# Reordered first loads and copies, later memory turns, two modulation units in the cross attention, and a low part between two norm tiles

## The chip, the cores and the metric

One core of a Trainium2 chip runs the whole program. The time is the device time of one execution in microseconds; the median of several executions is compared. Engines are TensorE (PE, with its weight loads PEld), VectorE (DVE), ScalarE (ACT), GpSimd (POOL) and SyncE (SP), which here only issues transfers.

## The reference

The program computes three transformer blocks on 256 tokens of width 1024, all in float32. Two layers of the first kind come first, then one of the second kind:

```python
for l in range(2):
    h = rms_norm(x, pre_mix_g[l])
    x = x + rms_norm(parallel_mixer(h, ...), post_mix_g[l])      # LRU, 8 forgetting heads, 4 retention heads
    h = rms_norm(x, pre_cross_g[l])
    x = x + rms_norm(memory_cross_attention(h, mem_n, ...), post_cross_g[l])   # mem_n = rms_norm(mem, mem_norm_g)
    h = rms_norm(x, pre_ffn_g[l])
    x = x + rms_norm(swiglu(h, w_gate[l], w_up[l], w_down[l]), post_ffn_g[l])
mod = silu(c) @ w_ada + b_ada        # six vectors of 1024 that shift, scale and gate the last block
...                                  # windowed attention and spatial gating, then 16 experts, 32 tokens each
```

The vector `mod` needs nothing of x. Its matrix of 1024 x 6144 is read during the first two layers.

## The kernel before, in words

**Units.** In the first half the weights come in units of 128 x 2048 floats (1 MiB). A unit goes through four hands. SP loads it into one of four slots W (L2335, `load_unit`). ScalarE copies it to the format of the fast product, the high part WH (L974). VectorE subtracts that from W, which gives the low part WL (L1493). TensorE multiplies: activations too are kept as a high and a low part, and each product is three (high by high, high by low, low by high), 48 of 256 columns or 24 of 512 to a unit. WH and WL have two buffers each, so the high part of unit m waits until TensorE is done with unit m - 2. A slot is free again once the low part is made.

**Order.** No scheduler runs: each engine has its own program, and the order is what the Python code of that engine calls. `unit()` on ScalarE and VectorE makes the parts of the present and the next unit, if they aren't made (`ahead`), and then advances the side jobs by two steps (`beside.step(2)`); TensorE advances them by one step after each half of a unit. A side job is a generator; each `yield` ends its step. Two lanes run side by side: one has the forget gates and then the recurrence, the other the parameters (8 steps) and then the norm and turning of the memory (`norming`, L402, L1022, L1538). A step of one engine can wait for the same job's step on another, and everything that follows on that engine waits too.

**Norms.** A norm of X is: squares with row sums (ScalarE), mean square (VectorE), its power -1/2 (GpSimd), scaling of each of two 128-row tiles, half by VectorE and half by ScalarE, then 16 transposes on TensorE (L398 in steps, L422 at once), whose results ScalarE and VectorE store as high and low parts (L1019, L1488), eight chunks each. `post_norm` (L1547) does the other side for each tile: y times gain, times the root, plus X (L1557, L1488). It is followed by one to four units of keys or values of the memory (`FILL`, `norm_after`), beside which the next norm runs.

**Start.** SP issues X, the identity, the parameters, units 0, 1 and 2, three small tables (positions, forget bias, sink), the other constants, the memory, and then unit 3 and on. ScalarE does squares, scaling, the high parts of units 0 and 1 (`high(0)`, `early()`), and then the stores of the turned norm, for which it needs the parameters. VectorE waits for the identity and makes the one-hot column (two casts), then does its part of the norm, the low part of unit 0, and the low parts of the norm.

**Cross attention** (L644, L1241, L1885). Four query units, then four output units `w_co`. Around them go the scores of heads 0 to 3 (i = 0 to 3), their turning one step later, and the product with the values two steps later. VectorE does the maxima and probabilities of head i, then, for i of 4 and 5, two steps of `modulation` each, then the low parts of the units, then the low half of the values' result.

**Modulation** (L1564). Twelve of the 24 units of `w_ada_2` per layer are handled on VectorE: one multiplication and seven multiply-adds of 128 x 256 elements, in four steps of two. Loads go to two buffers AW and wait until the unit two before is done (L2346). They stand in SP's queue between the weight units: units 0 and 1 of a layer in the cross attention, unit n + 2 after the n-th feed-forward step. Unit 0 of a layer is computed in the cross attention, unit n + 1 in feed-forward step n: two of the eight operations after each of two weight units, two between the halves of the hidden product and two before its second half (L1923; from step 2 on another weight unit comes in between).

**Second half.** The experts' weights come in 192 loads of 2816 KB into six buffers. They are not split in parts. The first six wait for places in memory that the first half frees, the others for the buffer's last product.

Of the kernel before, what the change touches and what calls it, by code (L numbers as in the profile page):

```python
# [62 lines left out]
NW = 4  # L63
# [241 lines left out]
def tensor_program(e, C):  # L305
# [93 lines left out]
            ins.then_inc(*up("full", "turn", name, k0))  # L399
            yield  # L400

    def norming(name, rows=M.XN1):  # L402
        yield
        e.wait_ge(*at("scaled_first", name, 1))
        e.wait_ge(*at("scaled_second", name, 1))
        yield from turning(name, [rows[:, 0, :], rows[:, 1, :]], 8)
# [58 lines left out]
    def mixer(l):  # L465
# [31 lines left out]
        proj_t("w_in", l, 1, HT, ("ly", l))  # L497
        fg, rec = forget(), recurrence()
        beside.add(fg, rec)
        memory = norming(("mem",), M.XN)  # L500
        if l == 0:
            beside.add(parameters(), memory, lane=1)
        proj_t("w_in", l, 2, HT, ("q", l, 0))
# [199 lines left out]
    def ffn(l):  # L703
# [17 lines left out]
        ada_sum(12 * l + 11)  # L721
        down(10)

    pre_norm(("mix", 0))
    for l in range(2):
        mixer(l)
# [230 lines left out]
def scalar_program(e, C):  # L957
# [8 lines left out]
    def par(name, i=0, n=1):  # L966
        a = PC[name][0] + i
        return M.PT[:, a:a + n]
# [13 lines left out]
    def early():  # L982
        m = here + 1
        if m < len(units) and m not in done:
            high(m)
# [33 lines left out]
                e.activation(dst[0][:, first + k, :], ps[:, k - k0, :], ACT.Identity, scale=g).then_inc(*up("hi", name, k))  # L1019
            yield  # L1020

    def norming(name, gain, ready, src=X, dst=HT, rows=M.XN1):  # L1022
        squares(name, src, ready)
        yield
        scaled(name, src, rows)
        yield from turning(name, dst, 0, 8, gain)

    def run_all(job):
# [61 lines left out]
    def mixer(l):  # L1090
# [63 lines left out]
        fg, rec = forget(), recurrence()  # L1154
        beside.add(fg, rec)
        if l == 0:
            memory = norming(("mem",), par("mem", 0, 8), ("mem",), M.XN, MEM, M.XN)
            beside.add(parameters(), memory, lane=1)
        unit()
        q_out(0)  # L1160
# [147 lines left out]
    scaled(("mix", 0))  # L1308
    high(0)
    here = 0  # L1310
    early()
    e.wait_ge(*at("par"))
    run_all(turning(("mix", 0), HT, 0, 8, par("pre_mix0", 0, 8)))
    for l in range(2):
        mixer(l)
        post_squares(("mix", l))
        norm_after(("post_mix", l), norming(("cross", l), par(f"pre_cross{l}", 0, 8), ("x", "mix", l)), l)
        cross(l)
        post_squares(("cross", l))
        norm_after(("post_cross", l), norming(("ffn", l), par(f"pre_ffn{l}", 0, 8), ("x", "cross", l)), 1)  # L1320
        ffn(l)
        post_squares(("ffn", l))
        if l == 0:
            norm_after(("post_ffn", 0), norming(("mix", 1), par("pre_mix1", 0, 8), ("x", "ffn", 0)), 1)
# [140 lines left out]
def vector_program(e, C):  # L1465
# [69 lines left out]
            ins.then_inc(*freed("turn", name, k0))  # L1535
            yield

    def norming(name, gain, dst=HT, *rows):  # L1538
        norm_head(name, *rows)
        yield  # L1540
        yield from turning(name, dst, 0, 8, gain)

    def run_all(job):
        for _ in job:
            pass

    def post_norm(y, gain, src=None, tmp=M.TMP):  # L1547
        for t in range(2):
            for h in range(2):
                if h:  # L1550
                    mean_square(y, at("ysq", *y, t, 1), t, "pms")
                else:
                    e.wait_ge(*at("ysq", *y, t, 0))
                c = slice(512 * h, 512 * h + 512)
                i = PS[:, 2 * t + h, :] if src is None else src[:, t, c]
                g = gain[:, c]
                e.tensor_tensor(tmp[:, t, c], i, g, ALU.mult).then_inc(*up("yfree", *y, t, h))  # L1557
            e.wait_ge(*at("prs", *y, t))
            for h in range(2):
                c = slice(512 * h, 512 * h + 512)  # L1560
                e.wait_ge(*at("yfree", *y, t, h))
                stt(X[:, t, c], tmp[:, t, c], K["rs2"][:, t:t + 1], X[:, t, c], ALU.mult, ALU.add).then_inc(*up("x", *y, t, h))
# [116 lines left out]
    def mixer(l):  # L1679
# [86 lines left out]
        fg, rec = forget(), recurrence()  # L1766
        beside.add(fg, rec)
        if l == 0:
            memory = norming(("mem",), par("mem", 0, 8), MEM, M.XN, M.XN)
            beside.add(parameters(), memory, lane=1)  # L1770
        for _ in range(3):
            unit()
# [112 lines left out]
    def cross(l):  # L1885
        def scores(h):
            P, col = M.PP[h % 3], 2 * h
            ps = two(full("cs", l, h))
            e.tensor_reduce(K["mxx"][:, col:col + 2], ps, AX.X, ALU.max).then_inc(*step())
            own()  # L1890
            ts(K["nmx"][:, col:col + 2], K["mxx"][:, col:col + 2], -1.0, None, ALU.mult).then_inc(*up("cnmx", l, h))
            e.wait_ge(*free("cs", l, h))
            e.reciprocal(K["rcp"][:, col:col + 2], K["sms"][:, col:col + 2]).then_inc(*step())
            own()
            for t in range(2):
                o = P[:, 256 * t:256 * t + 256]
                ins = ts(o, o, K["rcp"][:, col + t:col + t + 1], None, ALU.mult)
            ins.then_inc(*up("cprobs", l, h))

        def values(h):  # L1900
            ps = two(full("co", l, h))
            e.wait_ge(*at("co_high", l, h))
            e.tensor_tensor(MX[1][:, 2 * h:2 * h + 2, :], ps, MX[0][:, 2 * h:2 * h + 2, :].bitcast(F32), ALU.subtract).then_inc(
                *freed("co", l, h))

        unit()
        job = modulation(12 * l)
        for i in range(6):
            if i < 4:
                scores(i)  # L1910
            else:
                next(job)
                next(job)
            if i + 1 < 4:
                unit()
            if i >= 4:
                unit()
            if i >= 2:
                values(i - 2)
        unit()  # L1920
        unit()

    def ffn(l):  # L1923
        for n in range(11):
            A, i = M.A[n % 2], n % 4
            job = modulation(12 * l + n + 1)
            unit()
            next(job)
            ada_sum(12 * l + n)
# [15 lines left out]
        ada_sum(12 * l + 11)  # L1945
        unit()

    e.wait_ge(*at("id"))
    for i in range(2):
        ins = e.tensor_copy(M.ONE[64 * i:64 * i + 64, :], M.ID[0:64, 0:8])  # L1950
    ins.then_inc(*up("one_hot"))
    nrm = norming(("mix", 0), par("pre_mix0", 0, 8))
    next(nrm)
    low(0)
    e.wait_ge(*at("par"))
    run_all(nrm)
    for l in range(2):
        mixer(l)
        e.wait_ge(*at("gb", "mix", l))
        post_norm(("mix", l), M.GB)  # L1960
        norm_after(("post_mix", l), norming(("cross", l), par(f"pre_cross{l}", 0, 8)))
        cross(l)
        e.wait_ge(*at("gb", "cross", l))
        post_norm(("cross", l), M.GB)
        norm_after(("post_cross", l), norming(("ffn", l), par(f"pre_ffn{l}", 0, 8)))
        ffn(l)
        e.wait_ge(*at("gb", "ffn", l))
        post_norm(("ffn", l), M.GB)
        if l == 0:
            norm_after(("post_ffn", 0), norming(("mix", 1), par("pre_mix1", 0, 8)))  # L1970
# [360 lines left out]
def sync_program(e, C, out):  # L2331
# [20 lines left out]
    for t in range(2):  # L2352
        e.dma_start(M.X[:, t, :], D["x"][0, 128 * t:128 * t + 128, :]).then_inc(*up(f"x{t}", by=16))
        for h in range(2):
            same(("x", t, h), (f"x{t}",))
    e.dma_start(M.CST[:, 0:128], D["consts"][:, 0:128]).then_inc(*up("id", by=16))
    e.dma_start(M.PT[:, :], D["params"]).then_inc(*up("par", by=16))
    for m in range(NW - 1):
        load_unit(m)
    e.dma_start(K["posf"].bitcast(I32), D["positions_t"]).then_inc(*up("sm", 0, by=16))  # L2360
    e.dma_start(K["bf"][0:8, :], D["fox_b_t"]).then_inc(*up("sm", 1, by=16))
    e.dma_start(K["snk"], D["sink_2"].broadcast_to([128, 8])).then_inc(*up("sm", by=16))
    e.dma_start(M.CST[:, 128:NCONST], D["consts"][:, 128:NCONST]).then_inc(*up("cst", by=16))
    for t in range(2):
        e.dma_start(M.XN[:, t, :], D["mem"][0, 128 * t:128 * t + 128, :]).then_inc(*up(f"mem{t}", by=16))
# [141 lines left out]
```

## Time and profile before

| | us |
|---|---|
| median of three runs | 2382.78 (2379.72 to 2384.42) |
| the profiled execution, its own time | 2379.06 |
| its span, first to last instruction | 2377.3 |
| TensorE busy | 1824.5 (77%) |
| VectorE busy | 808.5 (34%) |
| ScalarE busy | 531.3 (22%) |
| chain that ended last | DMA 49%, TensorE 41%, VectorE 5% |

A line of the profile says: busy time of a group, its mean in ns, then the idle time of the engine just before it and what ended that idle time. In the timeline, "[3.65 <-issue]" means that the engine did nothing for 3.65 us and then began with no releaser that the profile shows. "WL<-W,WH" is output and inputs.

### The profile page before, as it was taken

The numbers are of one execution on the slowest core, as the hardware profiler recorded it, in microseconds if no ns is written. First come the engines' busy times: TensorE is split into PE (matmuls) and PEld (weight loads), VectorE is DVE, ScalarE is ACT, GpSimd is POOL, SyncE is SP. The second block draws the span as 40 slices with busy tenths as digits, with TensorE's granted clock in tenths as the row PEclk, the third lists the DMA queues.
The fourth block names the chain that finished last, engine by engine and source line by source line (L and its number), as shares of the span: only waits on it lengthen the run. The fifth ranks groups of instructions, "written<-read, shape, count | busy, mean of one in ns | idle before, by whom it ended". The sixth has DMA issues, their size and how long they took to land.

```text
span 2377.3 us, 28602 instructions
## 1 busy us (share of the span) xinstructions
PE 1824.5 (77%) x12548; PEld 1178.4 (50%) x12548; DVE 808.5 (34%) x1229; ACT 531.3 (22%) x800; POOL 90.8 (4%) x140
## 2 busy tenths in 40 slices
PE   7998999999988998977666566666656665566665
PEld 6888889988888997864121111122111121111121
DVE  4655667656556777653010101001100110010002
ACT  5634533355454434441000000000000000000000
POOL 1200000012000000010000000000000000000000
PEclk9999999999999999977877788788877877877777
DMA  7345467754454776347999999999999999999996
GB/s 241 107 135 194 142 213 238 240 163 134 142 165 154 249 246 204 125 188 323 429 429 430 429 429 429 429 429 430 429 429 429 430 430 428 428 430 429 428 429 265
DMA packets 171067, 739.78 MB, mean 311 GB/s; under 512 B 6672, under 2 KB 133136, under 8 KB 146240
## 3 DMA queue, kind: packets, MB, share of 16 engines
q1 hardware_dynamic: 168592, 731.27, 77.3%
q0 software_dynamic: 2352, 6.69, 0.8%
q8 instruction: 99, 1.62, 0.3%
q14 instruction: 24, 0.20, 0.0%
HBM read 736.88 MB, written 1.05 MB: 310 GB/s over the span
## 4 chain that ended last, share of the span: by engine, by line
DMA 49%; PE 41%; DVE 5%; ACT 2%; issue 2%; POOL 1%; SPq 0%; POOLq 0%; DVEq 0%; ACTq 0%
PE PS L325 39%; DMA WB<-in_w_down 24%; DMA WB<-in_w_up 23%; DVE WL L1493 1%; ACT WH L974 1%; DVE X L1488 1%; DMA W<-in_w_gate 1%; POOL T L2234 1%; DVE C L1488 1%; DMA S<-in_post_mix_g 1%; PE PS L398 0%; DMA W<-in_w_in 0%; PE PS L422 0%; DVE S L1557 0%; DVE S L1488 0%
## 5 line engine op out<-in xcount | busy, mean ns | idle before, releaser
L325 PE MATMUL PS<-WB,XS 128*32 128x352 f32 x3072 | 363.5, 635 | 211.3 <-DMA WB<-in_w_up 124.2
L325 PE MATMUL PS<-WB,S 128*32 128x512 f32 x1408 | 268.8, 759 | 156.5 <-DMA WB<-in_w_down 78.8
L1493 DVE TENSOR_TENSOR WL<-W,WH 128x2048 fp32r<-128x2048 f32 x141 | 322.9, 2290 | 146.1 <-ACT WH L974 146.0
L325 PEld LDWEIGHTS PS<-WB,XS 128*32 128x32 f32 x3072 | 115.6, 141 | 456.6 <-issue 177.9
L1488 DVE SCALAR_TENSOR_TENSOR S<-S,PS 128x352 f32<-128x352 f32 (+1 forms) x110 | 63.3, 587 | 784.8 <-ACT S L1458 751.2
L325 PE MATMUL PS<-HTh,WH 128*128 128x256 f32 x1064 | 310.5, 292 | 18.8 <-DVE HTl L1488 8.4
L974 ACT ACTIVATE WH<-W 128x2048 fp32r<-128x2048 f32 x141 | 268.8, 1908 | 199.7 <-PE PS L325 186.7
L325 PE MATMUL PS<-HTl,WH 128*128 128x256 f32 x1064 | 305.0, 287 | 0.0
L325 PE MATMUL PS<-HTh,WL 128*128 128x256 f32 x1064 | 304.9, 287 | 0.0
L325 PEld LDWEIGHTS PS<-WB,S 128*32 128x32 f32 x1408 | 72.1, 127 | 342.2 <-issue 222.2
L325 PEld LDWEIGHTS PS<-HTh,WH 128*128 128x128 f32 x1064 | 208.3, 196 | 21.8 <-DVE WL L1493 10.4
L325 PEld LDWEIGHTS PS<-HTl,WH 128*128 128x128 f32 x1064 | 208.3, 196 | 1.0
L325 PEld LDWEIGHTS PS<-HTh,WL 128*128 128x128 f32 x1064 | 208.1, 196 | 0.0
L1453 ACT ACTIVATE S<-PS 128x256 f32<-128x256 f32 x16 | 6.1, 384 | 850.0 <-PE PS L887 850.0
L2223 DVE TENSOR_TENSOR N<-N,PS 128x512 f32<-128x512 f32 x60 | 41.2, 687 | 368.4 <-PE PS L325 368.4
L325 PE MATMUL PS<-C,XS 128*32 128x352 f32 x1024 | 111.5, 590 | 65.9 <-DMA C<-in_w_up 37.9
L325 PE MATMUL PS<-WH,MXh 128*128 128x512 f32 x336 | 134.5, 400 | 2.0 <-DVE MXl L1488 2.0
L325 PE MATMUL PS<-WL,MXh 128*128 128x512 f32 x336 | 132.0, 393 | 0.0
L325 PE MATMUL PS<-WH,MXl 128*128 128x512 f32 x336 | 132.0, 393 | 0.0
L325 PE MATMUL PS<-S 128*128 128x512 f32 (+3 forms) x288 | 102.8, 490 | 30.3 <-DVE S L2210 22.1
L325 PEld LDWEIGHTS PS<-C,XS 128*32 128x32 f32 x1024 | 36.5, 132 | 139.2 <-DMA C<-in_w_up 52.5
L1461 ACT ACTIVATE S<-PS 128x512 f32<-128x512 f32 x16 | 9.6, 597 | 378.1 <-PE PS L325 378.1
(269 smaller groups left out, 2105.3 us busy)
## 6 DMA issues: line engine op xcount, KB each, us to landing
WB<-in_w_down SPq DMA_DIRECT2D x64, 2816.0 KB, 36.0
WB<-in_w_gate SPq DMA_DIRECT2D x48, 2816.0 KB, 35.9
WB<-in_w_up SPq DMA_DIRECT2D x48, 2816.0 KB, 35.9
C<-in_w_gate SPq DMA_DIRECT2D x16, 2816.0 KB, 36.2
C<-in_w_up SPq DMA_DIRECT2D x16, 2816.0 KB, 37.2
W<-in_w_in SPq DMA_DIRECT2D x31, 1024.0 KB, 5.4
S<-in_w_ada SPq DMA_DIRECT2D x24, 1024.0 KB, 5.4
W<-in_w_gate SPq DMA_DIRECT2D x22, 1024.0 KB, 7.8
```

The costliest lines, as they stand in the source:

```text
L325: return e.matmul(o, l, r, start=start, stop=stop, skip_group_check=True)
L974: e.activation(M.WH[m % 2][:, :], M.W[:, 2048 * (m % NW):2048 * (m % NW) + 2048], ACT.Copy).then_inc(*up("high", m))
L1453: e.activation(M.SG[ex % 2], ps[:, 0:256], ACT.Copy).then_inc(*freed("sg", ex))
L1461: e.activation(M.DN[ex % 2][:, 0, :], PS[:, 4, :], ACT.Copy).then_inc(*up("dn0", ex))
L1488: return e.scalar_tensor_tensor(out=o, in0=a, scalar=s, in1=b, op0=o1, op1=o2)
L1493: e.tensor_tensor(M.WL[i][:, :], M.W[:, 2048 * (m % NW):2048 * (m % NW) + 2048], M.WH[i][:, :].bitcast(F32), ALU.subtract).then_inc(*up("l ...
L2223: e.tensor_tensor(o, o, ps, ALU.add).then_inc(*done_)
L2234: return e.tensor_tensor(o, i, K["mhalf"] if n == 1 else K["mhalf"].broadcast_to([128, n]), ALU.pow)
```

## The change

Five edits. (1) Start: SP issues unit 0 ahead of the parameters, the three small tables next, then waits for unit 0's landing before it issues units 1 and 2. ScalarE's `early()` (unit 1's high part) comes after the stores of the turned norm. VectorE's one-hot casts come after the norm's head and unit 0's low part. TensorE waits for the identity itself. (2) The memory's norm has two more empty steps between scaling and the first turning, on all three engines. (3) In layer 0, VectorE's `post_norm` after the mixer makes the low parts of the present and the next unit between its two tiles. (4) In the cross attention two modulation units are computed, two steps at each of i = 2, 3 (first unit) and 4, 5 (second). (5) In return feed-forward step 0 has none; steps 1 to 10 keep theirs. The order of the modulation loads in SP's queue is the same.

```diff
 # TensorE
-    def norming(name, rows=M.XN1):
-        yield
+    def norming(name, rows=M.XN1, pad=0):
+        for _ in range(1 + pad):
+            yield
-        memory = norming(("mem",), M.XN)
+        memory = norming(("mem",), M.XN, 2)
+    e.wait_ge(*at("id"))
     pre_norm(("mix", 0))
 # ScalarE
         squares(name, src, ready)
         yield
         scaled(name, src, rows)
+        for _ in range(pad):
+            yield
         yield from turning(name, dst, 0, 8, gain)
-            memory = norming(("mem",), par("mem", 0, 8), ("mem",), M.XN, MEM, M.XN)
+            memory = norming(("mem",), par("mem", 0, 8), ("mem",), M.XN, MEM, M.XN, 2)
     high(0)
-    early()
     e.wait_ge(*at("par"))
     run_all(turning(("mix", 0), HT, 0, 8, par("pre_mix0", 0, 8)))
+    early()
 # VectorE
-    def post_norm(y, gain, src=None, tmp=M.TMP):
+    def post_norm(y, gain, src=None, tmp=M.TMP, between=None):
         for t in range(2):
+            if t and between:
+                between()
-            memory = norming(("mem",), par("mem", 0, 8), MEM, M.XN, M.XN)
+            memory = norming(("mem",), par("mem", 0, 8), MEM, M.XN, M.XN, pad=2)
-        job = modulation(12 * l)
+        jobs = [modulation(12 * l + i) for i in range(2)]
         for i in range(6):
             if i < 4:
                 scores(i)
-            else:
-                next(job)
-                next(job)
+            if i >= 2:
+                for _ in range(2):
+                    next(jobs[i // 2 - 1])
-            job = modulation(12 * l + n + 1)
+            job = modulation(12 * l + n + 1) if n else iter(range(4))
+    nrm = norming(("mix", 0), par("pre_mix0", 0, 8))
+    next(nrm)
+    low(0)
     e.wait_ge(*at("id"))
     for i in range(2):
         ins = e.tensor_copy(M.ONE[64 * i:64 * i + 64, :], M.ID[0:64, 0:8])
     ins.then_inc(*up("one_hot"))
-    nrm = norming(("mix", 0), par("pre_mix0", 0, 8))
-    next(nrm)
-    low(0)
-        post_norm(("mix", l), M.GB)
+        post_norm(("mix", l), M.GB, between=None if l else ahead)
 # SP
     e.dma_start(M.CST[:, 0:128], D["consts"][:, 0:128]).then_inc(*up("id", by=16))
+    load_unit(0)
     e.dma_start(M.PT[:, :], D["params"]).then_inc(*up("par", by=16))
-    for m in range(NW - 1):
-        load_unit(m)
     (the three small tables)
+    e.wait_ge(*at("w0", 0))
+    for m in range(1, NW - 1):
+        load_unit(m)
```

## Rows read from the trace of the kernel before

**Rows 1.** Page, the span in 40 slices: busy tenths of TensorE and DMA.

```profile
PE   7998999999988998977666566666656665566665
DMA  7345467754454776347999999999999999999996
```

**Rows 2.** Chain of waits, 0 to 1100 us: start us, us, what.

```profile
190.14 14.66 PE PS L325 x120
306.52 8.02 DMA W<-in_w_gate
```

**Rows 3.** Timeline of ScalarE at the start: start us, us, instruction, count, idle before.

```profile
10.25 1.91 ACT L974 ACTIVATE WH<-W 128x2048 fp32r<-128x2048 f32 x1 [1.05 <-DMA W<-in_w_in]
13.26 1.91 ACT L974 ACTIVATE WH<-W 128x2048 fp32r<-128x2048 f32 x1 [1.10 <-DMA W<-in_w_in]
15.08 3.01 ACT L1019 ACTIVATE HTh<-PS,PT 128x256 fp32r<-128x256 f32 x8
```

**Rows 4.** Timeline of VectorE at the start.

```profile
5.98 0.34 DVE L1950 CAST ONE<-C 64x8 fp32r<-64x8 f32 x2 [5.98 <-DMA C<-in_consts]
...
12.19 2.29 DVE L1493 TENSOR_TENSOR WL<-W,WH 128x2048 fp32r<-128x2048 f32 x1 [3.23 <-ACT WH L974]
16.06 3.23 DVE L1488 SCALAR_TENSOR_TENSOR HTl<-PS,PT,HTh 128x256 fp32r<-128x256 f32 x8 [1.58 <-ACT HTh L1019]
```

**Rows 5.** Page, DMA issues: count, KB each, median us from issue to landing.

```profile
W<-in_w_in SPq DMA_DIRECT2D x31, 1024.0 KB, 5.4
```

**Rows 6.** Timeline of TensorE: its first product and five gaps in mid-stream.

```profile
17.08 0.55 PE L325 MATMUL PS<-HTh,WH 128*128 128x256 f32 x1 [5.61 <-DVE HTl L1488]
...
83.76 1.09 PE L398 MATMUL PS<-C,N 128*128 128x128 f32 x4 [3.65 <-issue]
...
190.14 0.39 PE L325 MATMUL PS<-WH,MEMh 128*128 128x256 f32 x1 [2.65 <-DVE WL L1493]
...
311.52 0.39 PE L325 MATMUL PS<-HTh,WH 128*128 128x256 f32 x1 [2.10 <-DVE WL L1493]
327.72 0.39 PE L325 MATMUL PS<-HTh,WH 128*128 128x256 f32 x1 [2.51 <-DVE WL L1493]
...
761.16 0.39 PE L325 MATMUL PS<-HTh,WH 128*128 128x256 f32 x1 [1.36 <-DVE WL L1493]
```

**Rows 7.** Stretches, TensorE alone: us, busy (x), granted clock, DMA share, GB/s.

```profile
83.40:86.80 3.40, 3.04 (x15) 0.50 0.86 283
312.10:315.50 3.40, 3.40 (x18) 0.50 1.09 350
```

**Rows 8.** Timelines of ScalarE and VectorE around the norm after mixer 0.

```profile
182.37 1.91 ACT L974 ACTIVATE WH<-W 128x2048 fp32r<-128x2048 f32 x1
...
189.03 1.90 ACT L974 ACTIVATE WH<-W 128x2048 fp32r<-128x2048 f32 x1
...
187.80 2.28 DVE L1493 TENSOR_TENSOR WL<-W,WH 128x2048 fp32r<-128x2048 f32 x1
...
192.43 2.28 DVE L1493 TENSOR_TENSOR WL<-W,WH 128x2048 fp32r<-128x2048 f32 x1
```

**Rows 9.** Timelines of VectorE and ScalarE in the cross attention of layer 0.

```profile
252.85 2.29 DVE L1493 TENSOR_TENSOR WL<-W,WH 128x2048 fp32r<-128x2048 f32 x1 [0.51 <-ACT WH L974]
...
257.64 0.60 ACT L1268 ACTIVATE MXh<-PS 128x512 fp32r<-128x512 f32 x1 [4.82 <-PE PS L325]
```

**Rows 10.** Timelines of VectorE and ScalarE in feed-forward step 0, layer 0.

```profile
304.04 2.04 DVE L1488 SCALAR_TENSOR_TENSOR C<-S,T,C 128x256 f32<-128x256 f32 x4
...
306.71 0.63 ACT L1301 ACTIVATE MXh<-S 128x512 fp32r<-128x512 f32 x1 [7.08 <-DVE S L1488]
...
314.56 1.91 ACT L974 ACTIVATE WH<-W 128x2048 fp32r<-128x2048 f32 x1 [5.42 <-DMA W<-in_w_gate]
```

**Rows 11.** Timeline of VectorE beside GpSimd work in the mixer of layer 0.

```profile
105.74 1.33 DVE L1485 TENSOR_SCALAR C<-C,T 128x128 f32<-128x128 f32 x2
...
109.83 0.29 DVE L1782 CUSTOM_DVE_ANT_0 C<-PS,C 128x128 f32<-128x128 f32 x1 [0.77 <-PE PS L325]
```

More of the change, by code:

```diff
@@ L1020, in turning, with norming @@
             yield
-    def norming(name, gain, ready, src=X, dst=HT, rows=M.XN1):
+    def norming(name, gain, ready, src=X, dst=HT, rows=M.XN1, pad=0):
         squares(name, src, ready)
@@ L1536, in turning, with norming @@
             yield
-    def norming(name, gain, dst=HT, *rows):
+    def norming(name, gain, dst=HT, *rows, pad=0):
         norm_head(name, *rows)
-        yield
+        for _ in range(1 + pad):
+            yield
         yield from turning(name, dst, 0, 8, gain)
```

## The prediction

> **What bounds the kernel now.** I read the page's slices first. From the 20th of 40 slices (1130 us) DMA is 9 tenths busy or more and TensorE 5 to 7; before, TensorE is mostly at 8 or 9 tenths and DMA at 3 to 7 [rows 1]. So the second half streams expert weights, and its start is set by TensorE's progress in the first half; a microsecond won before 1089 us should arrive whole at the end, because every expert load waits for a buffer that earlier work frees. Then I read the chain of waits for the first 1100 us. It is TensorE work (a long piece is shown), broken by short stretches that are not: two are the landing of a gate load, 8.0 us each, one per layer, of which the first is shown [rows 2]. Last, TensorE's own timeline: the idle ahead of its first product and of five later ones [rows 6]. The sum is over these gaps.
>
> **1. First unit.** ScalarE makes the high part of unit 0 when the load lands (10.25 to 12.16), then waits 1.10 us for unit 1, makes its high part, and only at 15.08 begins the turned norm [rows 3]. VectorE finishes the low part of unit 0 at 14.48 and idles 1.58 us until 16.06 for that norm [rows 4]. The product starts 1.02 us after, at 17.08 [rows 6].
> After: ahead of unit 0 in SP's queue the parameters (176 columns of 128 floats, 88 KB, 0.26 us at the 3.0 us in which the queue moves a MiB [rows 3]) are gone, so unit 0 lands at about 9.95. I count nothing for loads 1 and 2 no longer behind it: the landings that release the two high parts are 3.0 us apart, one unit at a time [rows 3], which is a queue served in order. High part to 11.85; norm on ScalarE at once, first pair at 12.6; low part on VectorE to 14.15; then the two one-hot casts, which the change moves behind the low part, 0.34 [rows 4]; norm's low parts from 14.45; product at 14.45 + 1.02 = 15.45. **Gain 1.6 us.** Bounds: 0, if something ahead of TensorE's turns is late, to 3.8, if the shorter gap (11 to 15.45 instead of 11.47 to 17.08) keeps the clock up.
> Cost of the wait on SP: unit 1 is issued at 10.0, not 3.1, with a median of 5.4 us to landing [rows 5], so 15.4; its high part then runs 15.4 to 17.3, its low part after VectorE's eight norm steps (14.45 + 3.23 = 17.7) to 20.0, and TensorE ends unit 0 at about 23. Behind the wait stand unit 2, the constants, the memory and all later loads, each about 2 us later than now. Their users are far off (unit 2's high part is made after unit 0 ends, the memory is normed some 50 us on), so I cost this at nothing; it would cost from a landing of unit 1 after 18.8 on. TensorE's new wait on the identity is free: it landed before 5.98 [rows 4].
>
> **2. Memory's turns.** After the first half of one unit TensorE has to turn the memory, but the scaled rows come at 83.7: it idles 3.65 us, and its four transposes take 1.09 us [rows 6]. The clock is at half, 1.2 GHz, from 83.4 to 86.8, behind this gap [rows 7]. With two more yields on TensorE, ScalarE and VectorE all three agree again, and the four visits move one unit later, from the visits in units 7 and 8 to those in 8 and 9. Scaling stays where it is, so it has 8 us more. A unit is 48 products of 0.122 us [rows 2], so unit 7, half done at 80.11, ends at about 83.2 with the gates between. What is late next: high part 9 on ScalarE (scaling until 83.7, gate, copy, 1.9) ends at about 87.4, low part 9 at 89.7, wanted at about 94. Two visits' VectorE work (4 x 0.44) move one unit on, to where VectorE idles only 0.77 us [rows 11]: its maxima come 1 us later, its low part too, with 3 us in hand. Unit 9 then starts 3.5 us earlier by the idle alone (3.65 less what the later transposes meet), and 1.7 more if the clock stays up. **Gain 5.2 us** (bounds 0, if the wait only reappears at the new place, to 5.4).
>
> **3. Low part between one norm's tiles (layer 0 only).** TensorE idles 2.65 us until 190.14 for a low part that starts at 187.80, though its high part was ready at 184.28 [rows 6, 8]. After: it starts at 185.1 and ends at 187.4, as TensorE ends the unit before (187.5). But the second tile of X is 2.28 us later; ScalarE squares it in front of the next high part, which moves from 189.03 to 191.3 and ends at 193.2; the next low part ends at 195.5 instead of 194.7, and TensorE, done with its unit at 193.3, waits for it. Before, that unit began at 196.0. So the stall moves by one unit. **Gain 0.4 us**, bounds -0.5 to 2.6.
>
> **4. Two modulation units in the cross attention (both layers).** Eight VectorE steps per layer (one product 0.35 and seven multiply-adds of 0.51, about 3.9 us) leave the first feed-forward step.
> In the feed-forward, VectorE puts four of those steps (304.04, 2.04) between the two halves of the hidden product, and ScalarE's copy follows at 306.71, then high part, then low part; TensorE idles 2.10 us for it [rows 6, 10]. Without the four steps the copy starts 1.96 earlier, at 304.8, the high part ends at 307.4, the low part at 309.65; TensorE is free at 309.42, so 0.25 us remain: **1.8 us**. The clock at half from 312.1 to 315.5 [rows 7] costs 1.7: 18 matmuls in 3.4 us, against 28 at full. It goes if the gap goes.
> Also SP: the fourth modulation load can't be issued before the last of the eight steps, with gate unit 2 behind it (306.52, landed 8.02 later), and ScalarE waits 5.42 us for that [rows 2, 10]. After, the modulation buffer is free since the cross attention, and the gate load goes out when its own slot is, in the norm before the feed-forward. That wait's cost is in the next gap: at 327.72, 2.51 us idle [rows 6]. The chain from the hidden product to the end of the next low part (0.6, four steps that stay 2.04, 0.6, copy 0.7, 1.9, 2.3: 8.1 us) runs against one unit and a modulation sum on TensorE, 6.1, and leaves 2.0. **Sum for layer 0: 1.85 + 1.7 + 0.5 = 4.0 us.** Layer 1 has the same figure (gap 1.36 at 761.16; clock at half behind it, gate load in the chain, like layer 0) [rows 6]: 1.36 + 1.7 + 0.5 = **3.6 us**. Bounds for each 0 (SP's queue or another wait takes over) to 5.
> In the cross attention the steps come behind the scores of heads 2 and 3. Behind head 2: low part of the first output unit 1.0 later, wanted 6 us later. Behind head 3: 2.04 before the low half of values 1, then 1.9 before the second output unit's low part, which starts at 254.2 instead of 252.85 and ends at 256.5. TensorE wants it once values 2 are done, at 257.6 [rows 9]. Margin 1.1 us: cost nothing, and one for one beyond.
>
> **Clock.** The three stretches at half clock cost 5.1 of the sum; rows show them behind gaps of 3.65, 2.10 and 1.36 us [rows 6, 7], while the gap of 2.65 us at 190.14 was followed by none (the 120 products from there ran at 0.122 us) [rows 2]. I take them as gone with their gaps.
> The Trainium skill, TensorE: Matmul & The Clock Gate, section "What's actually happening", holds that the moment of such a switch depends on where the work falls in a monitor that runs free of the program, so the same kernel differs from run to run. That the smaller gaps have a drop and the larger none agrees with it, and it makes the second rival below possible.
>
> **Sum.** 1.6 + 5.2 + 0.4 + 4.0 + 3.6 = 14.8 us. The profiled execution took 2379.06 us (span 2377.3), which makes 2364.3; but it was faster than all three timed runs, whose median is 2382.78. Nothing in the sum is special to it, so I take the sum from the median: **2368 us**.
>
> **Rivals.**
> - *Gaps go, clock does not come back* (it drops elsewhere as often): 14.8 - 5.1 = 9.7, so 2373. For: a drop after a gap of 1.36 and none after 2.65. Against: the gap of 3.65 is the longest in mid-stream.
> - *Memory's turns wait again at the new place*, or ScalarE and VectorE, 5 us closer to TensorE, become the bound there: 14.8 - 5.2 = 9.6, again 2373. For: VectorE is nearly full in that unit [rows 11]. Against: the margins of 3 us above.
> - *Hidden anyway*: the expert stream's start does not follow TensorE, or SP's reordered queue gives the time back: 2380 to 2384. Against: DMA is not full before the 20th slice [rows 1], and all that an expert load waits for is TensorE's or VectorE's progress.
> - *Slower*: VectorE in the cross attention. It decides at the second output unit's low part, from 1.1 us of delay. If the moved steps stretch as two small VectorE products did beside GpSimd work, 1.33 us for 0.55 [rows 11], 2.4 times, then the 12 steps ahead of that low part take 14 us instead of 5.8, and the four behind them 2.9 more: 8.2 - 1.1 + 2.9 = 10 us a layer, 20 in both; with the gains kept 2388. Against: GpSimd is idle there, and the same steps run at 0.51 in that place today.
>
> **Chances.** Forecast 0.58; clock 0.15; memory's turns 0.14; hidden 0.08; slower 0.05. Range: the forecast's own is 2362 to 2373 (start clock 2.2, and 3 us by which runs of one kernel differ); the second and third reach 2378; below, 2360. A difference under 0.2%, 4.8 us, can't be told from none. Faster is then below 2378.0: 0.87; within 0.08; slower 0.05.
>
> **What would show it.** Right: TensorE's first product near 15.4; no gap at 80 and no half clock there; a gap of about 2.2 us one unit after the first unit behind the mixer's norm; the first two gaps in each feed-forward 0 to 0.3 and about 2.0; no gate load in the chain; the first expert-stream load about 14 us earlier. Wrong: a new VectorE or ScalarE wait ahead of the second output unit, TensorE waiting for scaled memory rows in unit 8, or unit 1 landing after 18.8.

## The result, and the profile after

The changed kernel took 2366.57 us (median of four runs, 2366.04 to 2368.98); the kernel before, beside it, 2382.1. The ratio is 0.9938, with a 95% interval from 0.9926 to 0.9951: 11.7 to 17.6 us faster. Forecast were 2368 us and 14.8 us. The profiled execution took 2366.92 us (span 2365.1, 12.2 less than before's).

Of the page after, the same slices as [rows 1]: the second half is as full of DMA as it was, only shorter.

```profile
span 2365.1 us, 28603 instructions
PE   7999999999998998987666566666666665666565
DMA  7345657654445775357999999999999999999996
```

The chain of waits up to 1100 us (start, length, what it waited for), its longest pieces that are not TensorE work. The two gate loads of [rows 2] are no longer in it. What remains is the first weight, the gain of the norm behind each mixer, and in layer 1 a GpSimd step.

```profile
2.13 7.49 DMA W<-in_w_in
169.01 5.96 DMA S<-in_post_mix_g
628.28 3.66 POOL T L2241
636.54 5.73 DMA S<-in_post_mix_g
```

TensorE's timeline after (start, duration; in brackets the idle time before it and what ended it), where [rows 6] shows the gaps of before. The first product starts at 15.19 instead of 17.08. The memory's four transposes run at 87.46 with no idle ahead of them, where there were 3.65 us. The stall behind the mixer's norm is 2.09 at 188.22 instead of 2.65 at 190.14. In the first feed-forward step of layer 0, 2.10 and 2.51 became 0.27 and 2.10; in layer 1 the first gap is gone and the second is 1.36.

```profile
15.19 0.55 PE L325 MATMUL PS<-HTh,WH 128*128 128x256 f32 x1 [3.99 <-DVE HTl L1492]
...
87.46 0.60 PE L398 MATMUL PS<-C,N 128*128 128x128 f32 x4
...
188.22 0.39 PE L325 MATMUL PS<-WH,MEMh 128*128 128x256 f32 x1 [2.09 <-DVE WL L1497]
...
301.99 0.39 PE L325 MATMUL PS<-HTh,WH 128*128 128x256 f32 x1 [0.27 <-DVE WL L1497]
316.20 0.39 PE L325 MATMUL PS<-HTh,WH 128*128 128x256 f32 x1 [2.10 <-DVE WL L1497]
...
765.01 0.39 PE L325 MATMUL PS<-HTh,WH 128*128 128x256 f32 x1 [1.36 <-DVE WL L1497]
```

Windows of TensorE's clock after (length, then busy time and count of each engine's instructions, granted clock, DMA share, GB/s). At 80 to 84 us, where the memory's gap was, the clock is full, and it stays full up to the stall at 316, where [rows 7] has a half-clock stretch behind that gap. Behind the 2.10 at 316.20 it is at half. Two stretches belong to no stall on which the prediction worked: one after the norm behind layer 1's mixer, which before's profile did not have, and one in layer 1's cross attention, shown over 6.8 of its 10.2 us, where before's has 6.8.

```profile
80.00:84.00 4.00, 4.00 (x24) 2.85 (x23) 2.65 (x8) 3.90 (x8) 0.00 (x0) 1.00 0.48 158
188.20:191.60 3.40, 3.38 (x28) 3.38 (x29) 2.29 (x1) 0.36 (x1) 0.00 (x0) 1.00 0.70 214
316.80:320.20 3.40, 3.40 (x19) 3.40 (x18) 3.28 (x5) 0.00 (x0) 0.00 (x0) 0.50 1.09 349
654.70:658.10 3.40, 3.40 (x18) 3.40 (x17) 3.26 (x4) 0.99 (x1) 0.00 (x0) 0.50 0.68 270
726.40:733.20 6.80, 6.07 (x29) 5.70 (x28) 4.92 (x9) 3.03 (x8) 0.81 (x2) 0.50 0.66 231
```

The gain arrives at the end, as supposed. One line for SP's first gate loads of the experts, before and then after: the first is issued at 1001.5 instead of 1013.9, the last at 2255.9 instead of 2267.8. That is 12.4 and 11.9 us earlier, and the span is 12.2 shorter.

```profile
L2403 SPq DMA_DIRECT2D WB<-in_w_gate x48: 327/328/341, 1013.9 to 2267.8; - x48
```

```profile
L2412 SPq DMA_DIRECT2D WB<-in_w_gate x48: 327/328/341, 1001.5 to 2255.9; - x48
```

How far TensorE's k-th product lies ahead of the same product before, worked out from its records in the two traces, tells where the time came from:

| stretch of the kernel after | ahead by, us | new in it |
|---|---|---|
| first units (to 51 us) | 1.9 to 2.0 | start, 1.9 |
| behind the memory's turns (97 to 171) | 7.2 | 5.2 |
| behind the stall at 188 | 7.7 | 0.5 |
| layer 0 feed-forward, end of first step (from 363) | 11.5 | 3.8 |
| layer 1, behind the mixer's norm (687) | 10.5 | -1.0 |
| layer 1 cross attention (742) | 8.9 | -1.6 |
| layer 1 feed-forward (from 809) | 12.5 | 3.5 |

### The profile page after: what moved, and what is told of

Read it like the earlier page. It is cut to its first block, busy times and chain, and to the rows that moved or that the text cites. A ratio compares the mean times of both kernels' runs of the same rounds, so it can differ in the third digit from the quotient of the medians.

```text
span 2365.1 us, 28603 instructions
## 1 busy us (share of the span) xinstructions
PE 1822.1 (77%) x12548; PEld 1175.4 (50%) x12548; DVE 808.2 (34%) x1229; ACT 531.5 (22%) x800; POOL 90.6 (4%) x140
## 4 chain that ended last, share of the span: by engine, by line
DMA 48%; PE 41%; DVE 5%; ACT 3%; issue 2%; POOL 1%; SPq 0%; POOLq 0%; DVEq 0%; ACTq 0%
PE PS L325 40%; DMA WB<-in_w_down 24%; DMA WB<-in_w_up 23%; DVE WL L1497 1%; ACT WH L976 1%; DVE X L1492 1%; POOL T L2241 1%; DMA S<-in_post_mix_g 0%; PE PS L398 0%; PE PS L423 0%; DVE C L1492 0%; ACT HTh L1021 0%; DMA W<-in_w_in 0%; DVE S L1564 0%; DVE S L1492 0%
## 5 line engine op out<-in xcount | busy, mean ns | idle before, releaser
L325 PE MATMUL PS<-WB,XS 128*32 128x352 f32 x3072 | 357.2, 625 | 211.7 <-DMA WB<-in_w_up 125.4
L325 PE MATMUL PS<-HTh,WL 128*128 128x256 f32 x1064 | 304.8, 286 | 0.0
L325 PE MATMUL PS<-C,XS 128*32 128x352 f32 x1024 | 120.6, 631 | 67.1 <-DMA C<-in_w_up 40.3
```

What stands on the lines that cost most here:

```text
L325: return e.matmul(o, l, r, start=start, stop=stop, skip_group_check=True)
```

## The experiments

Medians in us; "before" is the kernel before, run beside each. A ratio compares the two and has its 95% interval; it need not be the quotient of the two medians to the last digit.

**One part of the change at a time: four kernels.**

*The start alone:* SP's order and its wait, TensorE's wait on the identity, VectorE's casts behind the low part, ScalarE's `early()` behind the turns.

```diff
-    for m in range(NW - 1):
-        load_unit(m)
+    load_unit(0)                       # ahead of the parameters
...
+    e.wait_ge(*at("w0", 0))
+    for m in range(1, NW - 1):
+        load_unit(m)
```

> The start's edits alone (unit 0 loaded first, wait for its landing, later high part of unit 1, later casts, the identity's wait). My theory, that the parts add up: TensorE's first product at 15.2 instead of 17.1, every later gap of before there at its old size (3.65 at the memory's turns, 2.1 and 2.5 in feed-forward 0), all 1.9 us earlier; median 2.0 us under before, 2380. Rival, that the start is given back because all loads are 2 us later: the gap at 45 grows or a DMA wait appears, and the time is that of before within 0.5 us.

Measured: 2379.8 against 2381.95, ratio 0.9994 (0.9986 to 1.0003). TensorE's first product starts at 14.89. The second row shows the memory's gap in full.

```profile
14.89 0.55 PE L325 MATMUL PS<-HTh,WH 128*128 128x256 f32 x1 [3.99 <-DVE HTl L1489]
...
81.56 0.63 PE L398 MATMUL PS<-C,N 128*128 128x128 f32 x4 [4.60 <-issue]
```

The ratio's interval reaches past 1, so the time alone does not show a gain. In the trace 2.1 us are won and kept until the stall near 188. That stall is followed by half clock (row below, same columns as above), as it was not in before's profile, and 0.8 us of the gain are left behind it.

```profile
187.80:191.20 3.40, 3.39 (x16) 3.39 (x17) 2.08 (x5) 0.79 (x1) 1.73 (x3) 0.53 0.64 217
```

*The memory's turns alone:*

```diff
-        memory = norming(("mem",), M.XN)
+        memory = norming(("mem",), M.XN, 2)     # pad=2, on all three engines
```

> The two empty steps in the memory's norm alone. My theory: the 3.65 us gap at 83.8 goes, no half clock right behind it, and everything behind unit 9 is 5.2 us earlier (3.5 of idle, 1.7 of clock); median 2377. Rival, that only the gap goes and the clock falls elsewhere: 3.5 us in the median, 2378.6. Rival, that the wait reappears in unit 8: nothing.

Measured: 2375.63 against 2381.95, ratio 0.9977 (0.9968 to 0.9986). The gap is gone and the products behind it run 5.2 us earlier, of which 1.5 go again to half clock behind the stall at 185:

```profile
185.80:189.20 3.40, 3.40 (x18) 3.40 (x18) 2.74 (x4) 0.00 (x0) 1.18 (x2) 0.50 0.99 319
```

*The low part between two tiles alone:*

```diff
-        post_norm(("mix", l), M.GB)
+        post_norm(("mix", l), M.GB, between=None if l else ahead)
```

> The low part between the two norm tiles of mixer 0 alone. My theory: the stall of 2.65 us ahead of the second unit goes and one of some 2.2 us comes ahead of the third, because ScalarE's squares of the late tile hold up its high part; 0.4 us gained behind it, nothing that the median can show (2382). Rival, that the removed stall is the gain: 2.6 us, 2379.5.

Measured: 2381.39 against 2381.95, ratio 0.9999 (0.999 to 1.0008). By the time it can't be told from before. The stall of 2.65 is gone, and one unit later stands another, of 2.10.

```profile
195.41 0.39 PE L325 MATMUL PS<-WH,MEMh 128*128 128x256 f32 x1 [2.10 <-DVE WL L1493]
```

*The modulation units alone:*

```diff
-        job = modulation(12 * l)
+        jobs = [modulation(12 * l + i) for i in range(2)]
...
-            job = modulation(12 * l + n + 1)
+            job = modulation(12 * l + n + 1) if n else iter(range(4))
```

> Two modulation units in the cross attention, none in feed-forward step 0, in both layers, alone. My theory: first gap of each feed-forward 0.3 and 0, second 2.1 and 1.4 to 2.0, no ScalarE wait for a gate load, no new gap at the second output unit; 3.8 us in layer 0 and 1.9 to 3.6 in layer 1 by what the clock does; median 7 us under before, 2375. Rival, VectorE late in the cross attention: a gap ahead of the second output unit in each layer, with less than 4 us gained in all. Rival, clock not gained: 4.1 us.

Measured: 2372.33 against 2381.95, ratio 0.9963 (0.9951 to 0.9976). The first gap of layer 0 is 0.26 and the next 2.10; layer 1 has no first gap and 1.36 at the next. TensorE's products gain 3.8 us in layer 0's feed-forward and 3.5 in layer 1's. ScalarE's high part of gate unit 2 waits for TensorE, not for its load, so SP's queue no longer holds it.

```profile
310.39 1.92 ACT L974 ACTIVATE WH<-W 128x2048 fp32r<-128x2048 f32 x1 [1.87 <-PE PS L325]
```

```profile
310.90 0.39 PE L325 MATMUL PS<-HTh,WH 128*128 128x256 f32 x1 [0.26 <-DVE WL L1493]
325.11 0.39 PE L325 MATMUL PS<-HTh,WH 128*128 128x256 f32 x1 [2.10 <-DVE WL L1493]
```

What follows: the product of the four ratios is 0.9933, that of the whole change 0.9938. By the ratios the parts add up, and at 2382 us they are 1.4, 5.5, 0.2 and 8.8 us. By the differences of the medians they are 2.2, 6.3, 0.6 and 9.6 us, 18.6 together, against 15.5 for the whole. The intervals leave room for both: added up by their squares they are about 4.7 us to either side (an estimate from the four intervals).

**Is the load order part of the start's gain?** The changed kernel with SP's transfers in their old order and no wait:

```diff
-    load_unit(0)
     e.dma_start(M.PT[:, :], D["params"]).then_inc(*up("par", by=16))
+    for m in range(NW - 1):
+        load_unit(m)
...
-    e.wait_ge(*at("w0", 0))
-    for m in range(1, NW - 1):
-        load_unit(m)
```

> The changed kernel with SP's first transfers in their old order and no wait on unit 0. The new order of the copies is kept. My theory, that the copies' order makes the gain and the loads' only 0.3 us of it: unit 0's high part at 10.0 to 10.25, first product at 15.5 to 15.8, 0.3 to 0.6 later than in the changed kernel. Rival, that unit 0 lands earlier for having nothing behind it: first product at 16.5 or later.

Measured: 2367.26 against 2381.25, ratio 0.9942 (0.9927 to 0.9957). The first product starts at 15.88, 0.7 us later than in the changed kernel, a little more than the 0.3 to 0.6 of the theory. But at 51 us TensorE is only 0.1 behind it, and it has caught up ahead of the first stall behind the start (45.02 against 44.88 us, 1.60 us of idle in both). The reason is the clock: this execution has 15 products at the slow rate before the clock rises, at 19.2 us, and the changed kernel's profile has 21, until 19.8. Whether that comes from the order or from the execution, one profile of each does not tell. In the median, 2367.26 against 2366.57 and 2366.75, the order of the loads is worth nothing that can be told. What the start gains for certain is the reordering on ScalarE and VectorE.

```profile
15.88 0.55 PE L325 MATMUL PS<-HTh,WH 128*128 128x256 f32 x1 [4.78 <-DVE HTl L1492]
```

**How large is the margin in the cross attention?** The changed kernel with eight products into a scratch tile on VectorE ahead of the second output unit's low part, in both layers:

```diff
+            if i == 4:
+                for _ in range(8):
+                    ts(M.D3, M.CST[:, 0:256], 1.0, None, ALU.mult).then_inc(*step())
+                    own()
```

> The changed kernel with eight more VectorE products of 128x256 (0.35 us each, 3.0 us with their waits, into a scratch that nobody reads) ahead of the second output unit's low part in each cross attention. My theory: the low part ends at 251.4, TensorE wants it at 249.9, so a gap of 1.5 us per layer at that unit, and 3 us in the median unless the clock falls too. Rival, that the modulation steps are already at the edge there: 3.0 us per layer.

Measured: 2371.12 against 2381.25, ratio 0.9949 (0.9932 to 0.9965). The eight products took 2.6 us with their waits, not 3.0: the low part starts at 249.11 instead of 246.49. TensorE now waits for it, 1.37 us in layer 0 and 1.36 in layer 1. Against the changed kernel its products behind that place are later by 1.6 us in each layer, a little more than the idle time that the profile gives. So of 2.6 us 1.0 was margin. In this profile a half-clock stretch from 768.5 on, at the stall that ends at 768.9, takes another 1.3 us, and the median is 4.4 to 4.6 us over the changed kernel's, against the 3 of the theory "unless the clock falls too".

```profile
246.49 2.59 DVE L1489 TENSOR_SCALAR C<-C 128x256 f32<-128x256 f32 x8
249.11 2.29 DVE L1497 TENSOR_TENSOR WL<-W,WH 128x2048 fp32r<-128x2048 f32 x1
...
251.55 0.47 PE L325 MATMUL PS<-WH,MXh 128*128 128x512 f32 x1 [1.37 <-DVE WL L1497]
...
704.34 0.47 PE L325 MATMUL PS<-WH,MXh 128*128 128x512 f32 x1 [1.36 <-DVE WL L1497]
```

**Does SP's queue alone cost anything?** The kernel before, with the fourth modulation load of each layer one weight unit later in SP's queue, so that gate unit 2 is not behind its wait; the eight VectorE steps stay. It was run once, and then again with eleven runs.

```diff
+            if n == 2:
+                C.units.order.append(("ada", 12 * l + 3))
...
-            if n < 10:
+            if n < 10 and n != 1:
```

> The kernel before, with one change in SP's queue: the modulation load that waited for feed-forward step 0 stands one weight unit later, behind gate unit 2. VectorE's order is that of before. It splits the gain of the modulation edit. My theory: ScalarE's wait of 5.4 us for the gate load goes in both layers, the first gap of each feed-forward stays (2.1 and 1.4), the second shrinks by 0.4 in layer 0; under 1 us in all. Rival, that the blocked queue was the main cost: 3 us or more, and the first gap gone too.

> The kernel before with only SP's queue changed (modulation load one weight unit later), timed, since its one run was 5 us under the median of before while its trace showed TensorE's work before the experts only 0.3 to 0.7 us earlier. My theory, that this run was a lucky one in the expert stream: 0.5 us in the median. Rival, that the blocked queue was most of the modulation edit's gain: 4 us or more.

Measured: 2375.98 (one run), then 2377.55 against 2381.03, ratio 0.9982 (0.9973 to 0.9991), so 2.1 to 6.4 us of the kernel's 2381, in the middle 4.3; the two medians differ by 3.5. Of the first expectation the trace is the theory's, for the first gap stays, and the time is the rival's (3 us or more). Of the second the time lies between 0.5 and 4, nearer to 4. ScalarE makes two high parts back to back at 306.41, so the load is no longer waited for. The two stalls ahead of TensorE are 2.10 each, and against [rows 6] only the second is shorter, by 0.41. In layer 1 the second went from 1.90 to 1.36.

```profile
306.41 3.85 ACT L976 ACTIVATE WH<-W 128x2048 fp32r<-128x2048 f32 x2
```

```profile
310.69 0.39 PE L325 MATMUL PS<-HTh,WH 128*128 128x256 f32 x1 [2.10 <-DVE WL L1495]
326.38 0.39 PE L325 MATMUL PS<-HTh,WH 128*128 128x256 f32 x1 [2.10 <-DVE WL L1495]
```

**Is the half clock a property of the kernel or of the execution?** The changed kernel once more, nothing edited.

> The changed kernel again, with more runs, to see whether the parts measured alone (2.2, 6.3, 0.6 and 9.6 us, 18.6 together) add up. My theory: they do within the uncertainty, 15 to 18 us under before; the gaps of TensorE are the same to 0.1 us as in the first trace, and what differs between executions is where the clock is at half. Rival, that the parts overlap: 12 us or less.

Measured: 2366.75 against 2381.03, ratio 0.9935 (0.9923 to 0.9948). Its stalls are those of the first profile to a tenth of a microsecond (2.10 at 187.02, 2.10 at 316.48, 1.36 at 762.39), but the clock behind them is not. It is at half behind the stall near 188 (18 products in 3.4 us, 28 in the first profile) and full at 654.7, the other way round from the windows above. As to whether the parts add up, the theory had 15 to 18 us: it is 14.3 by the medians and 15.5 by the ratio, whose interval (12.4 to 18.3 us) just leaves out the rival's 12.

```profile
188.20:191.60 3.40, 3.40 (x18) 3.40 (x17) 1.47 (x1) 0.00 (x0) 0.00 (x0) 0.51 1.01 336
654.70:658.10 3.40, 3.40 (x30) 3.38 (x29) 3.34 (x5) 1.35 (x1) 0.00 (x0) 1.00 0.72 286
```

**A better version.** Two of the remaining stalls have the same form: VectorE or ScalarE does something that can wait ahead of a low part that can't. In the norm ahead of layer 0's cross attention, ScalarE makes the third unit's high part between the squares of the two tiles, and VectorE its low part ahead of that norm. In the second feed-forward step (n = 1) the four modulation steps go behind the low half of the hidden product.

```diff
-    def squares(name, src, ready):
+    def squares(name, src, ready, between=None):
+            if t and between:
+                between()
...
+        norm_after(("post_mix", l), norming(("cross", l), par(f"pre_cross{l}", 0, 8), ("x", "mix", l), between=None if l else early), l)
...
+        if place == ("post_mix", 0):
+            ahead()
...
-            next(job)
+            if n != 1:
+                next(job)
...
+            if n == 1:
+                next(job)
+                next(job)
```

> The changed kernel and two more edits that its trace points to. (1) Mixer norm of layer 0: ScalarE makes the third unit's high part between the squares of the two tiles, VectorE its low part ahead of the next norm's head. (2) Feed-forward step 1: VectorE's four modulation steps come behind the hidden product instead of between its halves, where VectorE waits for ScalarE's high part. My theory: the gap of 2.1 at 188 goes (2.1 us); the gaps at 316 and 765 shrink from 2.1 and 1.4 to 0.3 or less, and the half clock behind 316 goes: 2.1 + 1.8 + 1.2 = 5.1 us of idle and up to 1.7 of clock; median 2361. Rival, that the waits move on by one unit again, as at 188: under 2 us.

Measured: **2357.63** against 2381.25, ratio 0.9899 (0.9884 to 0.9914). That is 9 us better than the changed kernel, and faster than both kernels. The forecast was 2361. The first edit works: ScalarE makes the high part at 179.80, VectorE the low part at 182.12, and the stall at 188 is gone. The second falls short of the expectation in layer 0, where 1.02 us remain; in layer 1, 0.29.

```profile
179.80 1.92 ACT L976 ACTIVATE WH<-W 128x2048 fp32r<-128x2048 f32 x1 [1.79 <-PE PS L325]
```

```profile
182.12 2.28 DVE L1499 TENSOR_TENSOR WL<-W,WH 128x2048 fp32r<-128x2048 f32 x1
...
307.90 2.04 DVE L1494 SCALAR_TENSOR_TENSOR C<-S,T,C 128x256 f32<-128x256 f32 x4
309.86 2.28 DVE L1499 TENSOR_TENSOR WL<-W,WH 128x2048 fp32r<-128x2048 f32 x1
```

```profile
312.19 0.38 PE L325 MATMUL PS<-HTh,WH 128*128 128x256 f32 x1 [1.02 <-DVE WL L1499]
...
759.98 0.39 PE L325 MATMUL PS<-HTh,WH 128*128 128x256 f32 x1 [0.29 <-DVE WL L1499]
```

VectorE's rows say why: the four steps, put behind the hidden product (307.90), still run just ahead of the next low part, and hold it until 309.86.

Against the changed kernel's profile, TensorE's products gain 2.4 us at the stall near 188, 2.5 in layer 0's feed-forward (1.5 of it clock) and 1.1 in layer 1's, and lose 1.5 to a half-clock stretch at 527.7. That is near the forecast. The spans differ by 7.7 us and the medians by 9; 2.8 us of the former come between 1000 and 1300 us, where the edits change nothing, and are not explained. The two edits were not timed apart.

## Why the prediction was right, and where it was not

The predicted mechanism was right: short waits of TensorE in the first half, most of them for VectorE's low parts, removed one by one, and an expert stream whose start follows TensorE. By the terms of the sum (trace: the table above; alone: the ratio times 2382 us):

| term | predicted | in the trace | alone |
|---|---|---|---|
| start | 1.6 | 1.9 | 1.4 |
| memory's turns | 5.2 | 5.2 | 5.5 |
| low part between tiles | 0.4 | 0.5 | 0.2 |
| feed-forward, layer 0 | 4.0 | 3.8 | 8.8 for both |
| feed-forward, layer 1 | 3.6 | 3.5 | |
| new half clock, layer 1 mixer norm | 0 | -1.0 | |
| half clock longer, layer 1 cross attention | 0 | -1.6 | |

- **Start.** Forecast 15.45, measured 15.19. Unit 0 landed at 9.62 instead of 9.95. ScalarE's wait of 1.10 us for unit 1 ahead of the norm [rows 3] is gone. The norm starts with the high part's end, and VectorE's low part, casts and norm follow as the prediction ordered them:

```profile
9.64 1.91 ACT L976 ACTIVATE WH<-W 128x2048 fp32r<-128x2048 f32 x1 [0.78 <-DMA W<-in_w_in]
11.46 3.02 ACT L1021 ACTIVATE HTh<-PS,PT 128x256 fp32r<-128x256 f32 x8
15.09 1.92 ACT L976 ACTIVATE WH<-W 128x2048 fp32r<-128x2048 f32 x1 [0.62 <-DMA W<-in_w_in]
```

```profile
11.59 2.29 DVE L1497 TENSOR_TENSOR WL<-W,WH 128x2048 fp32r<-128x2048 f32 x1 [2.96 <-ACT WH L976]
13.80 0.34 DVE L1960 CAST ONE<-C 64x8 fp32r<-64x8 f32 x2
14.17 3.23 DVE L1492 SCALAR_TENSOR_TENSOR HTl<-PS,PT,HTh 128x256 fp32r<-128x256 f32 x8
```

  Unit 1 landed at 15.07 (forecast 15.4), far from the 18.8 from which it would have cost. The better half of the bound, a start at full clock, did not come: until 19.8 the products still take 415 ns each (one every 0.21 us), 21 of them where before has 22.
- **Memory's turns.** Both halves came, 3.5 of idle time and 1.7 of clock. Nothing was late behind them. The rival that they would wait again is out, by this profile and by the kernel with this part alone.
- **Between the tiles.** As forecast, the stall moved by one unit, and 2.09 of it stayed. The order of the work is the predicted one: the second tile's squares (182.17) stand ahead of the high part (183.94), and that low part starts at 185.88. The last kernel shows that it could be had: the high part belongs between the squares as well, and its low part ahead of the next norm.
- **Feed-forward.** Gaps forecast at 0.25 and 2.0 were 0.27 and 2.10 in layer 0. Layer 1's were none and 1.36; there "about 2.0" was too much. The working of ScalarE's copy was 304.8, which less the 7.7 us that all is earlier here is 297.1; it is at 297.18:

```profile
297.18 0.63 ACT L1305 ACTIVATE MXh<-S 128x512 fp32r<-128x512 f32 x1 [5.25 <-DVE S L1492]
```

- **The term that was mis-sized: SP's queue.** I put the load freed by the modulation buffer at 0.5 us a layer, read from one gap (2.51 to 2.0). As idle time of TensorE that is right: alone, it took 0.41 us off the gap in layer 0 and 0.54 in layer 1. In the time it gave 3.5 to 4.3 us alone, and at least 2.1 by the interval, against 1.0 in the sum. Where the rest is stays open. The two profiles of that kernel do not agree: one has a span of 2377.2, with before's at 2377.3, the other 2374.2. In the latter TensorE is 0.3 us ahead of before at 1010 us and 3.1 at 1160, so what it gained came behind the feed-forwards, where the experts' first loads and products are, and not at the gate load.
- **What the feed-forward term needs.** One thing can be argued from [rows 6, 7, 10], but is not shown. In before's profile the half clock at 312 slowed TensorE by 1.7 us. So it covered a gate unit whose low part was ready only at 318.8, while at full clock TensorE would have been done by 311.52 + 5.8 = 317.3. Two delays lay over each other there, and the sum had counted the clock's 1.7 as won by the removal of the gap alone; with the load still late some 1.5 of it would have gone to a wait. The total did not suffer, for the change removes both; no run removes the gap with the load still late. It does not explain the queue's 3.5 us alone, for there the half clock stayed.
- **The half clock.** The twelve profiles of this case, by the records of the granted clock, decide what the prediction had to guess from one:

| half clock behind | profiles with the gap | of these with the drop | profiles without the gap |
|---|---|---|---|
| memory's gap, 3.65 to 4.6 | 6 | 6 | 6, no drop |
| first feed-forward gap, layer 0, 2.1 | 6 | 6 | 6, no drop |
| second feed-forward gap, layer 0, 2.1 to 2.5 | 11 | 9 | 1 (1.02), no drop |
| stall at 185 to 195, 2.1 to 2.7 | 11 | 7 | 1, no drop |
| layer 1's mixer norm, 2.0 | 12 | 7 | |
| feed-forward gaps of layer 1, without the modulation edit, 1.36 and 1.4 to 1.9 | 6 | 6 | |
| the same with it, 1.36 alone | 5 | 2 | 1 (0.29), no drop |

  Two of the three stretches counted are tied to gaps that the change removes, so 3.4 of the 5.1 us was safe. The third was gone in the changed kernel's two profiles, but two of its variants still had it, so it was won in part. The rival "the clock doesn't come back" is out for those two places; what it fears happens at the other stalls, in some executions and not in others, whether the change is there or not. Half clock behind the second feed-forward gap [rows 6] was in before's profile too, and stays. One reading of the prediction was wrong: 3.65 us is not TensorE's longest gap in mid-stream. Before also has 5.67 at 735.4 and 5.95 at 946.3, and all twelve profiles have half clock around both. The forecast did not rest on it.
- **Profile and median.** The profiled gain is 12.2 us, the median's 15.5, and the sum of 14.8 lies between. The changed kernel's second profile has a span of 2362.3, 15.0 less than before's. Before's profile had no half clock behind its stall at 190, where seven other profiles had one, and none at 655 to 667; after's had the second. I had seen that it was quicker than the runs, and took the sum from the median all the same: from the profile it would have been 2364. That the median fell within 1.5 us of the forecast is in part luck: the sum left out the new drops of the clock, which took 2.6 us in the first profile, and it had the queue's term too small.
- **The slower side.** The moved steps ran as today, 0.51 us each (2.04 for four). The low part of the second output unit started at 246.22 and ended at 248.50, 1.06 us before TensorE began that unit:

```profile
241.84 2.04 DVE L1492 SCALAR_TENSOR_TENSOR C<-S,T,C 128x256 f32<-128x256 f32 x4
...
246.22 2.28 DVE L1497 TENSOR_TENSOR WL<-W,WH 128x2048 fp32r<-128x2048 f32 x1
```

```profile
249.56 0.58 PE L325 MATMUL PS<-WH,MXh 128*128 128x512 f32 x1
```

  The kernel with 2.6 us more on VectorE shows the mechanism of that rival at work, and that its price was well read: a margin of 1.1 us in the prediction and in these rows, and of 2.6 us of delay 1.6 came through, which is one for one beyond the margin.

## What to carry to other kernels

Where a second half streams at its limit and its start follows the first, read the bounding engine's stalls of 1 to 4 us one by one: those removed here were each an instruction of another engine, or a step of TensorE's own order, placed ahead of one that was wanted, and what decided was what that engine did in the few us ahead of the wanted one. Before you price one delay, ask what it covers: a half clock and a late load that lie over the same stretch hide each other in the trace (argued here from rows, not tested). Test a margin by putting known work ahead of the wanted instruction, and read from the rows how long that work was and how much later the bounding engine's products came; the idle time alone gave 1.37 of 1.6 us. Time kernels whose stalls are sometimes followed by half clock by medians of several runs, not by one profile's difference.

## What the hardware showed that I had not expected

- The same program, with the same stalls to 0.1 us, drops TensorE's clock behind different ones: behind the 2.1 us at 188 in one execution and not in another, with 18 and 28 products in the same 3.4 us. A drop of 3.4 us costs 1.2 to 1.7, and from 30 to 960 us the twelve profiles of this case have 27.3 to 41.0 us at half. In before's and in both of the changed kernel it is 34.1, 30.7 and 30.7. One drop, at 527.7 in the last kernel, came behind no stall longer than 0.96 us. The Trainium skill, TensorE: Matmul & The Clock Gate, section "What's actually happening", has the monitor run free of the program; that pair of profiles agrees.
- The profile's clock is only as good as its records. Up to 19.8 us of the changed kernel it shows full clock, and the products of that stretch take 415 ns and start every 0.21 us, where behind it they take 283 ns and start every 0.12 us.
- A load of 1 MiB that waits for its turn in the issuing queue, not for the wires, moved the median by 3.5 us over two layers, with its own stall visible in the trace at less than a third of that. In layer 0 it was issued at 306.52 behind the other load's wait, and at 286.16 without; from 300 to 304 us the DMA engines' busy share was 0.00 in both.
